# The last sixteen gate-stage blocks of an expert layer: four-pass fp32 products replaced by three fp32r passes, with the hi and lo parts made while the gates are summed

## The reference, cut to what matters

```python
s = jnp.einsum('thcd,cnd->thcn', q, sub_keys)          # 128 scores per head and half
# top 16 of each half, top 16 of their 256 sums -> idx (first*128 + second), gate = softmax
a = jnp.einsum('thkd,td->thk', down[ib], xb)
c = gb * jax.nn.gelu(a)
return jnp.einsum('thk,thkd->td', c, up[ib])
```

## Time and profile before

| | |
|---|---|
| median of 3 runs | 2864.52 us (2863.49 to 2865.87) |
| the profiled execution | 2863.67 us |
| its span, first to last instruction | 2861.8 us |
| TensorE busy | 2844.3 us, 99% |
| VectorE busy | 1882.3 us, 66% |
| ScalarE busy | 1369.6 us, 48% |
| GpSimd busy | 112.6 us, 4% |
| quarter 8 to the end of quarter 71, in each layer | 141.03 us |

### The profile page before, as it was taken

How to read it: one execution, slowest core, us unless ns; L and a number is a source line. 1 busy time by engine, 2 the same in 40 slices (tenths; PEclk the granted TensorE clock), 3 DMA queues, 4 the chain that set the end, 5 groups by cost and what they waited for, 6 DMA issues and landing times.

```text
span 2861.8 us, 44674 instructions
## 1 busy us (share of the span) xinstructions
PE 2844.3 (99%) x18054; PEld 2536.7 (89%) x18054; DVE 1882.3 (66%) x2946; ACT 1369.6 (48%) x1707; POOL 112.6 (4%) x81
## 2 busy tenths in 40 slices
PE   8999999999999999999999999999999999999998
PEld 7899888889999899988888999988899998888997
DVE  7889559655555788955866555566655556665664
ACT  6643334544444575333454444455455444545543
POOL 0033000000000002400000000000000000000000
PEclk9999999999999999999999999999999999999999
DMA  6344556765454534465676554456555656554663
GB/s 215 118 163 165 189 186 206 279 248 184 176 199 168 175 113 162 141 210 178 209 276 248 188 197 176 180 184 184 184 163 182 185 190 184 170 183 155 175 187 132
DMA packets 223375, 530.14 MB, mean 185 GB/s; under 512 B 13515, under 2 KB 87409, under 8 KB 211953
## 3 DMA queue, kind: packets, MB, share of 16 engines
q1 hardware_dynamic: 221872, 521.11, 54.7%
q0 software_dynamic: 1344, 6.82, 0.7%
HBM read 507.81 MB, written 20.06 MB: 184 GB/s over the span
## 4 chain that ended last, share of the span: by engine, by line
PE 98%; DVE 1%; DMA 0%; issue 0%; ACT 0%; SPq 0%; DVEq 0%
PE ps L2629 16%; PE ps L2611 13%; PE ps L1506 13%; PE ps L1516 12%; PE ps L1494 12%; PE ps L1434 9%; PE ps L1451 5%; PE ps L605 4%; PE ps L596 4%; PE ps L1423 2%; PE ps L2888 2%; PE ps L1224 1%; PE ps L2797 0%; PE ps L2781 0%; PE ps L1336 0%; PE ps L1403 0%
## 5 line engine op out<-in xcount | busy, mean ns | idle before, releaser
L2230 DVE TENSOR_TENSOR ring_lo<-ring,w_hi 128x1024 fp32r<-128x1024 f32 x320 | 388.4, 1224 | 242.6 <-ACT w_hi L2226 241.3
L2226 ACT ACTIVATE w_hi<-ring 128x1024 fp32r<-128x1024 f32 x320 | 335.2, 1056 | 235.3 <-PE ps L2629 168.7
L1434 PE MATMUL ps<-h_t,ring 128*128 128x256 f32 x1216 | 290.6, 385 | 0.0
L1506 PE MATMUL ps<-h_t_lo,down_hi 128*128 128x256 f32 x1024 | 288.5, 282 | 0.0
L1506 PE MATMUL ps<-h_t_expert,down_lo 128*128 128x256 f32 x1024 | 288.1, 281 | 0.0
L1506 PE MATMUL ps<-h_t_expert,down_hi 128*128 128x256 f32 x1024 | 287.1, 280 | 0.0
L2611 PE MATMUL ps<-h_t_lo,w_hi 128*128 128x256 f32 x928 | 261.1, 281 | 0.0
L2611 PE MATMUL ps<-h_t_hi,w_hi 128*128 128x256 f32 x928 | 259.7, 280 | 0.1
L2611 PE MATMUL ps<-h_t_hi,ring_lo 128*128 128x256 f32 x928 | 259.3, 279 | 0.0
L1434 PEld LDWEIGHTS ps<-h_t,ring 128*128 128x128 f32 x1216 | 221.2, 190 | 24.5
L1997 DVE TENSOR_TENSOR up_lo<-ring,up_hi 128x2048 fp32r<-128x2048 f32 x64 | 146.7, 2292 | 99.8 <-ACT up_hi L1101 99.8
(11 more groups left out here) (520 smaller groups left out, 6923.2 us busy)
## 6 DMA issues: line engine op xcount, KB each, us to landing
ring<-in_peer_down SPq DMA_DIRECT2D x128, 1024.0 KB, 5.2
ring<-in_w_in SPq DMA_DIRECT2D x140, 512.0 KB, 3.7
ring<-in_peer_up SPq DMA_DIRECT2D x68, 1024.0 KB, 4.7
ring<-in_w SPq DMA_DIRECT2D x132, 512.0 KB, 3.7
ring<-in_peer_up SPq DMA_DIRECT2D x120, 512.0 KB, 4.4
late_gates<-arena SPq DMA_DIRECT2D x64, 256.0 KB, 5.4
arena<-late_gates SPq DMA_DIRECT2D x16, 1024.0 KB, 7.5
ring<-in_w_out SPq DMA_DIRECT2D x16, 512.0 KB, 3.8
```

Of the source, the lines that this page charges most:

```text
L1434: m = pe.e.matmul(PS[:, act_bank(b), j * T:(j + 1) * T], lead_raw(b, j, RAW)[:, kc * P:(kc + 1) * P], HT[:, kc, :], start=kc == 0, stop=kc ...
L1506: m = pe.e.matmul(PS[:, 4 + b, j * T:(j + 1) * T], w[:, b, o], x[:, kc, :], start=kc == 0 and n == 0, stop=kc == KD - 1 and n == 2)
L2226: a.e.activation(W_HI[:, g % HI_SLOTS, :], RAW[:, g % RAW_SLOTS, :], ACT.Copy).then_inc(*a.count(f"c{g}_hi"))
L2230: v.e.tensor_tensor(RAW_LO[:, g % RAW_SLOTS, :], RAW[:, g % RAW_SLOTS, :], W_HI[:, g % HI_SLOTS, :].bitcast(F32), ALU.subtract).then_inc(* ...
```

## The change

- Blocks 16 to 31 go through `passes_quarter`. Their 32 halves are called turns, turn n = 2(b - 16) + j. High parts have three places: `OUT_LO[1]` and the two halves of ring place (1, 1). Turn n's high part waits for turn n - 3 to be multiplied. ScalarE makes it after `gates_out(s)` with s = max(0, 2n - 2) (`TURN_HIGH`).
- The low part of a turn is made by VectorE inside `hot(m)`, between the two remaining operations, m = n + 1 (2 for the first two turns, 31 for the last two; `TURN_LOW`).
- `hot(n)` has two operations of 128x2048 in place of four of 128x1024: both one-hots in one comparison, both gate parts in one multiplication with the mask broadcast. The comparison waits for sum 2n - 3. The tiles are rearranged and `hot_second0` moves to another place.
- Raw blocks 16 to 31 use three places, (1, 0), (0, 1), (0, 0) in turn; block 17 waits for block 15, block b from 19 on for block b - 3.
- `HT_EXPERT` is made by ScalarE at block 5 of stage 2, `HT_LO` by VectorE after `hot(3)`, once block 15 is multiplied; blocks 18 to 31 read these tokens.
- The 32 `late_out` stores are issued by GpSimd and no longer by SP. The first `up` block is loaded after block 31's load and after block 29 is multiplied, the second in two halves after block 30 and after the first half of block 31. `out_slot` is rotated by two, and the low part of `up` block 1 waits for the end of block 31.

The place of the sums (`QUARTER`) is as before: one after each of the quarters 5 to 68.

```diff
-LEAD_PLACE.update((b, (b % 2, 0)) for b in range(len(LEAD_LOADS), HELD + 2))
+LEAD_PLACE.update((b, ((0, 0), (1, 0), (0, 1))[b % 3]) for b in range(len(LEAD_LOADS), HELD))
+LEAD_PLACE.update((b, (b % 2, 0)) for b in range(HELD, HELD + 2))
+FIRST_TURN = GATE_SPLIT[-1] + 1
+OWN_X = FIRST_TURN + 2
+TURNS = 2 * (HELD - FIRST_TURN)
+TURN_HIGH = [next(s for s in range(SUMS) if QUARTER[s] >= 4 * (FIRST_TURN - LEAD) - 5 + 2 * n) for n in range(TURNS)]
+OWN_LOW = next(n for n in range(GROUPS_OF_TOKENS) if n >= 2 and QUARTER[2 * n - 3] >= 4 * (FIRST_TURN - LEAD))
+TURN_LOW = [min((s + 4) // 2, GROUPS_OF_TOKENS - 1) for s in TURN_HIGH]
...
+        def turn_free(n):
+            if n < 3 and turn_place(n) == 0:
+                last = max(2 * i + j for i in range(len(LEAD_SPLIT)) for j in range(2) if (2 * i + j) % LEAD_SLOTS == 1)
+                return f"act_half{LEAD_SPLIT[last // 2]}{last % 2}"
+            if n < 3:
+                return f"act_mm{[i for i in LEAD_LOADS if LEAD_PLACE[i] == (1, 1)][-1]}"
+            return f"act_half{FIRST_TURN + (n - 3) // 2}{(n - 3) % 2}"
...
             for b in range(LEAD):
+                if b == 5:
+                    a.e.activation(HT_EXPERT[:, :, :], HT[:, :, :], ACT.Copy).then_inc(*a.count("ht_hi"))
...
+            lead_high(a, LEAD + 1, (1,))
+            for s in range(SUMS):
+                gates_out(s)
+                if s < SUMS - 1:
+                    acts_out(s)
+                for n in range(TURNS):
+                    if TURN_HIGH[n] == s:
+                        lead_high(a, FIRST_TURN + n // 2, (n % 2,))
...
-                if b == 0 or b in LEAD_SPLIT or b in GATE_SPLIT:
+                if b == 0 or b in LEAD_SPLIT or b in GATE_SPLIT or b >= FIRST_TURN:
+                    if b == OWN_X and q == 0:
+                        pe.e.wait_ge(*pe.at("ht_lo"))
                     passes_quarter(b, q)
...
-                v.e.tensor_tensor(paired(MASK[:, n % 2, :, :]), pairs, each(HK_SECOND[:, at:at + GROUP, :]), ALU.is_equal)
                 if n >= 2:
                     v.e.wait_ge(*v.at(f"sum{2 * n - 3}"))
-                v.e.tensor_tensor(paired(HOT1[:, n % 2, :, :]), pairs, each(HK_FIRST[:, at:at + GROUP, :]), ALU.is_equal)
-                v.e.wait_ge(*v.at(f"mask{n}"))
-                for part in range(2):
-                    v.e.tensor_tensor(paired(HOT2[n % 2][:, :, part, :]), paired(MASK[:, n % 2, :, :]),
-                                      each(PARTS[:, part, at:at + GROUP, :]), ALU.mult)
+                v.e.tensor_tensor(HOT_KEYS[:, n % 2, :, :, :].rearrange("p c j (a b) -> p (c j) a b", b=2), numbers,
+                                  both(HK_BOTH[:, n, :, :, :]), ALU.is_equal).then_inc(*v.count(f"hot_keys{n}"))
+                for i in range(TURNS):
+                    if TURN_LOW[i] == n:
+                        lead_low(v, FIRST_TURN + i // 2, i % 2)
+                v.e.wait_ge(*v.at(f"hot_keys{n}"))
+                mask = HOT_KEYS[:, n % 2, 1, :, :].rearrange("p j (a b) -> p j a b", b=2)
+                v.e.tensor_tensor(HOT2[n % 2][:, :, :, :].rearrange("p c j (a b) -> p c j a b", b=2),
+                                  mask.unsqueeze(1).broadcast_to([P, 2, GROUP, P // 2, 2]),
+                                  PARTS[:, n, :, :, :].unsqueeze(3).broadcast_to([P, 2, GROUP, P // 2, 2]), ALU.mult)
...
+                if n == OWN_LOW:
+                    v.e.wait_ge(*v.at("ht_hi"))
+                    v.e.wait_ge(*v.at(f"act_mm{FIRST_TURN - 1}"))
+                    v.e.tensor_tensor(HT_LO[:, :, :], HT[:, :, :], HT_EXPERT[:, :, :].bitcast(F32), ALU.subtract)
...
+                for n in range(GROUPS_OF_TOKENS):
+                    p.e.wait_ge(*p.at(f"gates{2 * n + 1}"))
+                    p.e.dma_start(late_gates[:, n * GROUP * 64:(n + 1) * GROUP * 64], ARENA[:, late_stage(n):late_stage(n) + GROUP * 64])
...
-                    if b == len(LEAD_LOADS) + 1:
-                        for slot in range(2):
-                            last = max(i for i in LEAD_LOADS if LEAD_PLACE[i] == (slot, 1))
-                            sp.e.wait_ge(*sp.at(f"act_mm{last}"))
-                            peer_block(sp, "up", slot, slot, l, f"up_in{slot}")
+                    if b == HELD - 1:
+                        last = [i for i in LOADS if LEAD_PLACE[i] == (0, 1)][-1]
+                        sp.e.wait_ge(*sp.at(f"act_mm{last}"))
+                        peer_block(sp, "up", 0, 0, l, "up_in0")
+                    if b == HELD:
+                        for j in range(2):
+                            sp.e.wait_ge(*sp.at(f"act_half{HELD - 2 + j}{1 - j}"))
+                            held_up(sp, l, 1, j, f"dma_w{6 + j}")
```

More of the change, by code:

```diff
@@ L360, in build @@
             pass
-        with nc.sbuf_tensor("hot_first", [P, 2, GROUP, P], F16) as HOT1, \
-                nc.sbuf_tensor("hot_mask", [P, 2, GROUP, P], F16) as MASK:
+        with nc.sbuf_tensor("hot_keys", [P, 2, 2, GROUP, P], F16) as HOT_KEYS, \
+                nc.sbuf_tensor("hot_second0", [P, 2, GROUP, P], F16) as HOT2_EVEN:
             pass
@@ L620, in lead_slot_free @@
         def lead_slot_free(b, j):
+            if b >= FIRST_TURN:
+                return turn_free(turn_of(b, j))
             if b == 0:
@@ L678, in peer_block, with held_up @@
             sp.e.dma_start(view, ap).then_inc(*sp.count(name, f"dma_{which}{slot}"))
+        def held_up(sp, l, b, j, landed):
+            ap = bass.AP(tensor=dram["peer_up"].tensor, offset=l * (NKEYS * NKEYS * D) + b * (2 * D) + j * D,
+                         ap=[[NKEYS * D, P], [1, D]])
+            sp.e.dma_start(up_raw(b, j), ap).then_inc(*sp.count(f"up_in{b}{j}", landed))
         def late_stage(n):
@@ L1422, in sums @@
                     for part in range(2):
-                        m = pe.e.matmul(PS[:, GATE_BANKS[s % banks], j * P:(j + 1) * P], HOT1[:, n % 2, k, :],
-                                        HOT2[n % 2][:, k, part, :], start=part == 0, stop=part == 1)
+                        m = pe.e.matmul(PS[:, GATE_BANKS[s % banks], j * P:(j + 1) * P], HOT_KEYS[:, n % 2, 0, k, :],
+                                        HOT2[n % 2][:, part, k, :], start=part == 0, stop=part == 1)
                 m.then_inc(*pe.count(f"sum{s}"))
@@ L1449, in passes_quarter @@
                     o = slice(kc * P, (kc + 1) * P)
-                    for n, (w, x) in enumerate(((hi, LEAD_X_HI), (hi, LEAD_X_LO), (lo, LEAD_X_HI))):
+                    x_hi, x_lo = (LEAD_X_HI, LEAD_X_LO) if b < OWN_X else (HT_EXPERT, HT_LO)
+                    for n, (w, x) in enumerate(((hi, x_hi), (hi, x_lo), (lo, x_hi))):
                         m = pe.e.matmul(PS[:, act_bank(b), j * T:(j + 1) * T], w[:, o], x[:, kc, :],
@@ L1984, in hybrid_vector @@
                     lead_low(v, LEAD + 1, 1)
+                if n == OWN_LOW:
+                    v.e.wait_ge(*v.at("ht_hi"))
+                    v.e.wait_ge(*v.at(f"act_mm{FIRST_TURN - 1}"))
+                    v.e.tensor_tensor(HT_LO[:, :, :], HT[:, :, :], HT_EXPERT[:, :, :].bitcast(F32), ALU.subtract) \
+                        .then_inc(*v.count("ht_lo"))
             v.e.wait_ge(*v.at(f"gates{SUMS - 1}"))
@@ L2014, in hybrid_vector @@
                     fold(2 * b + 2, 2)
-                if b == HELD - 10:
-                    v.e.wait_ge(*v.at("ht_hi"))
-                    v.e.tensor_tensor(HT_LO[:, :, :], HT[:, :, :], HT_EXPERT[:, :, :].bitcast(F32), ALU.subtract) \
-                        .then_inc(*v.count("ht_lo"))
                 if b in (HELD - 7, HELD - 4):
```

79 lines of the change are left out of this document (29 added, 50 removed).

## The result

The changed kernel takes 2835.61 us (median of 4 runs, 2834.57 to 2836.82) against 2864.01 for the kernel before in the same comparison: a ratio of 0.990, 95% interval 0.9883 to 0.9917. It is faster, by 28.4 us. The forecast was 2835, in a range of 2828 to 2846.

A forecast was written before the change was run, and what follows sets the result against it. TensorE was taken as the bound, with 98% of the span: 2863.67 - 36.6 gained + 7.4 of waits = 2834.4 us profiled, 2835.2 for the median, stated as 2835. The range was 2828 to 2846.

The forecast's parts named there:

- TensorE's gain: Rewritten stage: steps of 1.94 instead of 2.229 us and a shorter tail save 18.32 us a layer, 36.6 for both.
- VectorE's group: VectorE's work for one group in the stage: 1.15 + 1.16 + 1.15 = 3.46 us, against 3.88 in TensorE's two steps.
- R3: Slower: the fused multiplication, last in each `hot(n)`, leaves the fast rate, a group takes 4.5 us; 2874 us; chance 0.08.
- (a): TensorE waits 0.6 us before block 16, whose low parts stand in `hot(2)` behind a comparison that waits for sum 1.
- (b): TensorE waits 0.6 us at sum 6: block 17's load lands late, `hot(3)`'s multiplication stands behind its low part.
- (c): TensorE waits 1.8 us at sum 8, as `HT_LO` stands ahead of `hot(4)` on VectorE.
- (d): TensorE waits 0.7 us at sum 62: `hot(31)` has two low parts, the second's high part comes after gates 60.
- Edits at nothing: `HT_EXPERT` copy moved to stage 2, ScalarE's work in the stage, later block loads and `up` loads: priced at nothing.
- R2: GpSimd's store issues shut out VectorE: a group takes 4.03 against 3.88 us, 8 us in all, 2843 us; chance 0.12.
- R4: Slower: GpSimd takes one store at a time, 6 us each against 3.88 a group; 2936 us; chance 0.03.
- R1: Fewer waits: VectorE hides (a) to (d) in part; bound with none 2828 us; chance 0.07.
- R5: Late loads in each block and VectorE at 4.3 us a group eat the gain; within 0.2%; chance 0.04.

The follow-up runs named there:

- the last two kernels: Changed kernel with low parts after the multiplication in every group, 2830.99 us; the same plus later token split and block 16's parts early, 2830.18 us.
- two single repairs: Changed kernel with block 17 loaded into block 14's place, 2836.18 us; separately, changed kernel with block 16's high and low parts made earlier, 2835.47 us.

## Why the prediction was right

**TensorE's gain.** 2.229 to 1.94 a step was to be 17.64 a layer; the 53 steps without a wait are 1.94 each. The tail was to be 4.82 and is 4.77. "If TensorE never waits" the gain is 18.4 a layer by the trace (145.36 less 126.9), forecast 18.32. The kernel without the passes shows that it is theirs alone.

The gain is less than the count of passes suggests. The Trainium skill ("FP8 and Floating Point Precision", TensorE Precision Notes) says that true fp32 takes four passes. Without sums a plain quarter takes (5.50 - 0.43) / 3 = 1.69; three quarters of that are 1.27, and the trace has (4.77 - 0.43) / 3 = 1.45. No row counts the passes of the plain form. So one pass less of four saves 14% here and not 25%.

**VectorE's group.** 3.46 forecast with 0.1 of hand-offs beside it, 3.50 measured. The fused operation starts the next after 1.14, between the bounds 1.11 and 1.22 and close to the 1.15 taken, and far from the 2.2 of R3. That all-16-bit rule ("VectorE: DVE Perf Modes" in the Trainium skill, What auto-detection actually checks, as cited in the forecast) holds for the mask repeated over parts too: 2048 elements of fp16 take 1.22, as long as 1024 of fp32.

**The waits.** All four are where they were forecast, and in this stage there is no other. Sizes, forecast against idle time shown: (a) 0.6 and 0.60, (b) 0.6 and 0.53, (c) 1.8 and 1.56, (d) 0.7 and 0.68. Their sum is 3.4 as idle time and 4.0 as lost time against 3.7: each pays 0.15 to 0.18 more than it shows, which the forecast left out. Each cause has its kernel: the late load and the order behind it (b), the split behind that delay (c), the last low part (d), and for (a) the early parts.

(b) is near by luck as well. Its due time, 289.9, has (a) in it; by its own rows it is 290.0 (281.66 + 0.6 + 4 x 1.94), and the wait 0.5. In the trace both ends of the sum are later: the gates of sum 6 are ready 9.27 after sum 2, where 8.84 was forecast, and TensorE could begin it at 8.74, where 8.24 was. The two errors of 0.4 to 0.5 cancel.

The forecast did not say how the waits hang together. (b) is small only since (a) came first; taken singly, (a) is worth nothing, the late load of block 17 comes back at block 29 at its full 1.3 and more, and only (c) and (d) can be had one by one. The order of multiplication and low part, which removes three of them, is not in the forecast.

**Edits at nothing.** Right: 2864.25 against 2863.95 with them and no passes. The first `up` blocks are in time, and the tail of 4.77 has no wait. The load of `up` block 2 had no term in the forecast: in one of two profiles of the changed kernel it costs 1.7 us in stage 4.

**The stores.** Priced nothing, right. Their landing was not: 4 to 7 was forecast, and the median is 2.7. The line of the stores gives the duration (ns, min/median/max, first and last start), then from issue to landing (us):

```profile
L896 POOL DMA_DIRECT2D late_gates<-arena x64: 540/540/579, 282.4 to 1329.2; - x64
...
DMA to landing us min/median/max: 2.3/2.7/8.2
```

R2 fell. The sixty-four issues took 540 ns, the longest 579. One stands at 323.55 on GpSimd's timeline, within the comparison of 322.66, and that comparison takes the 1.22 of all others:

```profile
323.55 0.54 POOL L896 DMA_DIRECT2D late_gates<-arena  x1 [3.29 <-ACT arena L1113]
```

The rule of the Trainium skill ("SBUF — State Buffer", Summary: rules for kernel authors) that such issues are starved beside VectorE's doubled modes is not borne out here, for operations of two tensors. Its figure for such a DMA ("DMA: Bandwidth & Descriptors", Anatomy of one DMA, GpSimd path), 2.0 us and the bytes at 436 GB/s, gives an estimate of 2.6 for 256 KB, and the trace has 2.7.

R4 (a store takes 6 us) fell with the landing of 2.7. R3 fell with the 1.14; the price that it set on a longer group is real, as the doubled multiplication shows. R1 (fewer waits) did not come of itself, but it is what the last two kernels reach by another order: 2831 and 2830. R5 did not occur.

## What to carry to other kernels

A busy share of 88% does not say where the waits are; the due time of each result does, and four waits could be placed to a few tenths by writing down for each what stands ahead of it in its queue. Put the result that is due soonest ahead of work that itself waits for a load: to turn two operations round removed three waits of four, at the price of a longer first one, where two single repairs won nothing, because the next wait stood in series or the late load moved on. To price a wait that follows another, add the delay that the first has already given to its due time.

## What was not expected of the hardware

**TensorE's clock after a wait.** In the kernel with block 17's place changed, windows of 5 us around the wait at sum 54 (columns as in the earlier trace rows; the eighth is the granted clock):

```profile
380.00:385.00 5.00, 4.24 (x44) 3.94 (x42) 1.17 (x2) 2.11 (x4) 0.27 (x1) 1.00 0.72 291
385.00:390.00 5.00, 3.60 (x29) 3.51 (x30) 4.77 (x6) 3.41 (x6) 0.81 (x2) 0.77 0.92 277
390.00:395.00 5.00, 5.00 (x47) 4.89 (x47) 4.06 (x4) 2.70 (x4) 0.54 (x1) 0.89 0.25 95
395.00:400.00 5.00, 5.00 (x56) 4.86 (x55) 4.62 (x5) 2.53 (x5) 1.08 (x2) 1.00 0.64 174
```

TensorE was idle 2.15, then worked for a while at the lower level, 1.2 GHz, before 2.4 came back; the means of the windows are 0.77 and 0.89. A sum's eight matmuls last 1.08 there for 0.62, and two steps take 2.46 and 2.96: 1.5 us on top of the 2.15. The doubled multiplication shows it too, 0.66 in 300 to 305 us after a wait of 2.84, and again at its sum 62, after a wait of 1.94 in each layer; the next step is 3.21 and 3.47 there:

```profile
425.00:430.00 5.00, 4.04 (x29) 3.95 (x30) 0.90 (x1) 1.09 (x2) 0.00 (x0) 0.66 0.91 338
```

After waits of 1.89 and 1.80 (block 16's parts early), of 1.86 (low part last, both layers) and of 1.78, 1.67 and 1.56 the following steps are 1.94. That is what these few cases show, and no rule can be read off them.

**GpSimd's stores land sooner.** 2.7 against 5.6 from SP, for the same 256 KB in the same stage, and 5.4 before the change. SP's queue holds the 1 MB loads, GpSimd's in the sums' time only these stores; which part of the difference is the queue and which the way of issuing was not tried.
